# Other start addresses for the split weight buffers of a two-block float32 transformer kernel

## What is computed

```python
def first_block(x, ...):
    for i in range(DEPTH):
        h = rmsnorm(x, norm_mix[i])
        x = x + (even_mixer(h, ...) if i % 2 == 0 else odd_mixer(h, ...))
        x = x + conv_ffn(rmsnorm(x, norm_ffn[i]), ...)

def second_block(x, ...):
    for layer in range(DEPTH):
        x = x + hybrid_mixer(rmsnorm_2(x, norm1[layer]), ...)
        h = rmsnorm_2(x, norm2[layer])
        x = x + (swiglu(h, ...) if layer % 2 == 0 else moe_swiglu(h, ...))
```

## Time and profile before

| what | value |
|---|---|
| median of 2 runs | 1558.99 us (1557.62 to 1560.37) |
| the profiled execution, first to last instruction (span) | 1558.8 us |
| instructions | 26842, of them 9894 matmuls |
| PE busy | 1525.1 us (98%) |
| DVE busy | 1188.6 us (76%) |
| ACT busy | 1017.6 us (65%) |
| DMA | 351 MB, mean 225 GB/s |

### The profile page before, as it was taken

One profiled execution on the slowest core, in us unless ns is written; L12 is line 12 of the kernel. 1 busy time (PEld: TensorE's weight loads), 2 busy tenths in 40 slices (PEclk: granted clock), 3 DMA queues, 4 the chain that ended last, 5 costly groups with the idle time before them and its releaser, 6 DMA issues.

```text
span 1558.8 us, 26842 instructions
## 1 busy us (share of the span) xinstructions
PE 1525.1 (98%) x9894; PEld 1308.5 (84%) x9894; DVE 1188.6 (76%) x1477; ACT 1017.6 (65%) x1431; POOL 60.4 (4%) x74
## 2 busy tenths in 40 slices
PE   7999999999999999999999999999999999999998
PEld 6988888878878888899888888998878888888886
DVE  5677877775578877787775556887688888888887
ACT  5667665566567656687465455875577777777775
POOL 0000000000000000020000000100000001101000
PEclk9999999999999999999999999999999999999999
DMA  7535455445424555464255555462699999999995
GB/s 269 195 119 189 167 211 188 177 147 189 169 102 165 213 188 184 142 190 144 80 192 187 204 181 184 162 167 83 227 373 368 394 387 381 369 396 385 364 362 210
DMA packets 54794, 351.08 MB, mean 225 GB/s; under 512 B 6208, under 2 KB 9968, under 8 KB 14896
## 3 DMA queue, kind: packets, MB, share of 16 engines
q1 hardware_dynamic: 46512, 330.94, 56.8%
q0 software_dynamic: 8192, 18.90, 4.7%
HBM read 341.90 MB, written 7.91 MB: 224 GB/s over the span
## 4 chain that ended last, share of the span: by engine, by line
PE 91%; DVE 4%; DMA 2%; ACT 2%; issue 1%; POOL 0%; SPq 0%; DVEq 0%; ACTq 0%
PE PS L917 20%; PE PS L1852 16%; PE PS L1985 14%; PE PS L2021 11%; PE PS L1870 8%; PE PS L1986 8%; PE PS L1478 1%; DVE EWL L3761 1%; PE PS L1083 1%; PE PS L1956 1%; DMA rows_m<-HN 1%; PE PS L1833 1%; DMA W<-in_weights 1%; PE PS L962 1%; PE PS L1547 1%
## 5 line engine op out<-in xcount | busy, mean ns | idle before, releaser
L3761 DVE TENSOR_TENSOR EWL<-W,EWH 128x2048 fp32r<-128x2048 f32 x144 | 329.6, 2291 | 45.4 <-ACT EWH L2789 45.2
L1985 PE MATMUL PS<-HTB,WH 128*128 128x512 f32 x944 | 329.3, 393 | 0.0
L2789 ACT ACTIVATE EWH<-W 128x2048 fp32r<-128x2048 f32 x144 | 276.5, 1920 | 61.3 <-PE PS L1870 34.2
L1986 PE MATMUL PS<-HTB,WL 128*128 128x256 f32 x1008 | 282.4, 280 | 0.0
L3087 DVE TENSOR_TENSOR WL<-W,WH 128x2048 fp32r<-128x2048 f32 x99 | 226.5, 2287 | 35.9 <-ACT WH L2216 32.8
L2216 ACT ACTIVATE WH<-W 128x2048 fp32r<-128x2048 f32 x99 | 189.2, 1918 | 95.4 <-PE PS L1986 84.6
L917 PE MATMUL PS<-MWH,HTB 128*128 128x256 f32 (+1 forms) x940 | 240.9, 341 | 2.1 <-issue 1.5
L3095 DVE TENSOR_TENSOR MWL<-W,MWH 128x1024 fp32r<-128x1024 f32 x136 | 164.5, 1220 | 85.2 <-ACT MWH L2240 83.2
L1985 PEld LDWEIGHTS PS<-HTB,WH 128*128 128x128 f32 x944 | 177.2, 188 | 40.1
L2240 ACT ACTIVATE MWH<-W 128x1024 fp32r<-128x1024 f32 x136 | 142.5, 1054 | 98.2 <-PE PS L917 89.8
L1986 PEld LDWEIGHTS PS<-HTB,WL 128*128 128x128 f32 x1008 | 189.5, 188 | 1.0
(11 more groups left out here) (413 smaller groups left out, 2441.1 us busy)
## 6 DMA issues: line engine op xcount, KB each, us to landing
W<-in_weights SPq DMA_DIRECT2D x311, 1024.0 KB, 4.9
CS<-in_consts POOLq DMA_DIRECT2D x4, 403.5 KB, 4.8
ARENA<-rows_m POOLq DMA_DIRECT2D x8, 192.0 KB, 6.2
ARENA<-rows_m POOLq DMA_DIRECT2D x2, 768.0 KB, 12.2
moe_acc<-X POOLq DMA_DIRECT2D x3, 512.0 KB, 12.1
moe_rows<-HN POOLq DMA_DIRECT2D x3, 512.0 KB, 12.1
X<-in_x SPq DMA_DIRECT2D x2, 512.0 KB, 4.4
W<-in_weights SPq DMA_DIRECT2D x2, 512.0 KB, 7.1
```

Source lines behind the costliest of these rows:

```text
L1985: mm(PS[b][:, :], WH[:, sl, o:o + P], HTB[:, :, kk, :], start=(kk == 0), stop=False, skip_group_check=True)
L1986: ins = mm(PS[b][:, 0:256], WL[:, sl, o:o + P], HTH[:, kk, :], start=False, stop=(kk == KC - 1), skip_group_check=True)
L2789: A(EWH[tile % SPLIT][:, :], tile_ap(w0 + tile), ACT.Copy).then_inc(sem("moe_hi"), 1)
L3761: TT(EWL[tile % SPLIT][:, :], tile_ap(w0 + tile), EWH[tile % SPLIT][:, :].bitcast(F32), SUB).then_inc(sem("moe_lo"), 1)
```

## The change

Every split buffer gets a start of its own within 64 bytes. `shifted` allocates a buffer with 16 elements (64 bytes) of room and gives back the part that begins `by` elements in. The tuples are in elements of 4 bytes, one entry for each of the three buffers:

```diff
+SHIFT_ROOM = 16
+MIXER_SHIFT, FFN_SHIFT, MOE_SHIFT = (2, 4, 12), (12, 12, 4), (4, 6, 1)
...
+    nc.alloc_sbuf_tensor("HTB_END", [P, 2 * SHIFT_ROOM], F32)
     W = nc.alloc_sbuf_tensor("W", [P, RING, KC * TW], F32)
+    nc.alloc_sbuf_tensor("W_END", [P, 2 * SPLIT * SHIFT_ROOM], F32)
...
-    ARENA_N = 21632
+    ARENA_N = 21632 + 6 * SHIFT_ROOM
...
-    MWH = nc.alloc_sbuf_tensor_at("MWH", [P, SPLIT, HALF], F32R, offset=mw_at)
-    MWL = nc.alloc_sbuf_tensor_at("MWL", [P, SPLIT, HALF], F32R, offset=mw_at + 4 * SPLIT * HALF)
+    def shifted(name, n, at, by):
+        return nc.alloc_sbuf_tensor_at(name, [P, n + SHIFT_ROOM], F32R, offset=at)[:, by:by + n]
+    half_step = 4 * (HALF + SHIFT_ROOM)
+    MWH = [shifted(f"MWH{k}", HALF, mw_at + k * half_step, MIXER_SHIFT[k]) for k in range(SPLIT)]
+    MWL = [shifted(f"MWL{k}", HALF, mw_at + (SPLIT + k) * half_step, MIXER_SHIFT[k]) for k in range(SPLIT)]
...
+    WH = [shifted(f"WH{k}", KC * TW, wh_at + k * tile_step, FFN_SHIFT[k]) for k in range(SPLIT)]
+    WL = [shifted(f"WL{k}", KC * TW, wl_at + k * tile_step, FFN_SHIFT[k]) for k in range(SPLIT)]
...
-    EWH = [nc.alloc_sbuf_tensor_at(f"EWH{k}", [P, TILE_N], F32R, offset=o) for k, o in enumerate(moe_hi_at)]
-    EWL = [nc.alloc_sbuf_tensor_at(f"EWL{k}", [P, TILE_N], F32R, offset=o) for k, o in enumerate(moe_lo_at)]
+    EWH = [shifted(f"EWH{k}", TILE_N, o, MOE_SHIFT[k]) for k, o in enumerate(moe_hi_at)]
+    EWL = [shifted(f"EWL{k}", TILE_N, o, MOE_SHIFT[k]) for k, o in enumerate(moe_lo_at)]
```

More of the change, by code:

```diff
@@ L171, in build @@
     HT = nc.alloc_sbuf_tensor_at("HT", [P, KC, S], F32, offset=ht_at)
-    MWH = nc.alloc_sbuf_tensor_at("MWH", [P, SPLIT, HALF], F32R, offset=mw_at)
-    MWL = nc.alloc_sbuf_tensor_at("MWL", [P, SPLIT, HALF], F32R, offset=mw_at + 4 * SPLIT * HALF)
-    assert 2 * SPLIT * HALF <= (RING - RAW) * KC * TW
+    def shifted(name, n, at, by):
[3 more added lines that the diff above has]
+    MWL = [shifted(f"MWL{k}", HALF, mw_at + (SPLIT + k) * half_step, MIXER_SHIFT[k]) for k in range(SPLIT)]
+    assert 2 * SPLIT * HALF <= (RING - RAW) * KC * TW and max(MIXER_SHIFT + FFN_SHIFT + MOE_SHIFT) <= SHIFT_ROOM
     ff_n = 6 * 2 * 512
-    gh_n, wh_n = 2 * 512, SPLIT * KC * TW
+    gh_n, wh_n = 2 * 512, SPLIT * (KC * TW + SHIFT_ROOM)
     assert ff_n + 2 * gh_n + 2 * wh_n <= ARENA_N
@@ L179, in build @@
     GHL = nc.alloc_sbuf_tensor_at("GHL", [P, 2, 2, S], F32R, offset=arena_at + 4 * (ff_n + gh_n))
-    WH = nc.alloc_sbuf_tensor_at("WH", [P, SPLIT, KC * TW], F32R, offset=arena_at + 4 * (ff_n + 2 * gh_n))
-    WL = nc.alloc_sbuf_tensor_at("WL", [P, SPLIT, KC * TW], F32R, offset=arena_at + 4 * (ff_n + 2 * gh_n + wh_n))
-    WL1_AT = ff_n + 2 * gh_n + wh_n + KC * TW
+    tile_step = 4 * (KC * TW + SHIFT_ROOM)
+    wh_at, wl_at = arena_at + 4 * (ff_n + 2 * gh_n), arena_at + 4 * (ff_n + 2 * gh_n + wh_n)
+    WH = [shifted(f"WH{k}", KC * TW, wh_at + k * tile_step, FFN_SHIFT[k]) for k in range(SPLIT)]
+    WL = [shifted(f"WL{k}", KC * TW, wl_at + k * tile_step, FFN_SHIFT[k]) for k in range(SPLIT)]
+    WL1_AT = ff_n + 2 * gh_n + wh_n + KC * TW + SHIFT_ROOM
     TILE_N, sel_n, gr_n, xs_n = KC * TW, NT * N_EXP * P, 2 * 256, 2 * KC * P
     dead_at = -(-(cs_at + 4 * CST["reset"][0]) // 32) * 32
-    assert dead_at + 8 * TILE_N <= cs_at + 4 * (CST["pool"][0] + CST["pool"][1])
+    step_n = TILE_N + SHIFT_ROOM
+    assert dead_at + 8 * step_n <= cs_at + 4 * (CST["pool"][0] + CST["pool"][1])
     SELR = nc.alloc_sbuf_tensor_at("SELR", [P, NT, N_EXP, P], F32R, offset=arena_at)
     moe_hi_at = [dead_at, ht_at, arena_at]
-    moe_lo_at = [dead_at + 4 * TILE_N, htl_at, arena_at + 4 * TILE_N]
-    EWH = [nc.alloc_sbuf_tensor_at(f"EWH{k}", [P, TILE_N], F32R, offset=o) for k, o in enumerate(moe_hi_at)]
-    EWL = [nc.alloc_sbuf_tensor_at(f"EWL{k}", [P, TILE_N], F32R, offset=o) for k, o in enumerate(moe_lo_at)]
-    moe_at = arena_at + 4 * 2 * TILE_N
+    moe_lo_at = [dead_at + 4 * step_n, ht_at + 4 * step_n, arena_at + 4 * step_n]
+    EWH = [shifted(f"EWH{k}", TILE_N, o, MOE_SHIFT[k]) for k, o in enumerate(moe_hi_at)]
+    EWL = [shifted(f"EWL{k}", TILE_N, o, MOE_SHIFT[k]) for k, o in enumerate(moe_lo_at)]
+    moe_at = arena_at + 4 * 2 * step_n
     GRH = nc.alloc_sbuf_tensor_at("GRH", [P, 2, 256], F32R, offset=moe_at)
@@ L204, in build @@
     GAT = nc.alloc_sbuf_tensor_at("GAT", [P, NT, GAT_W], F32R, offset=moe_at + 4 * (2 * gr_n + 2 * xs_n + S))
-    moe_n = 2 * TILE_N + 2 * gr_n + 2 * xs_n + S + gat_n
+    moe_n = 2 * step_n + 2 * gr_n + 2 * xs_n + S + gat_n
     sel_at = -(-mx_at // 32) * 32
@@ L209, in build @@
     GAIN = nc.alloc_sbuf_tensor_at("GAIN", [P, D], F32, offset=sel_at)
-    YL = [nc.alloc_sbuf_tensor_at(f"YL{k}", [P, D // 2], F32R, offset=o) for k, o in enumerate((sel_at + 4 * D, dead_at + 8 * TILE_N))]
-    assert sel_at + 6 * D <= mx_at + 4 * N_MX and dead_at + 8 * TILE_N + 2 * D <= cs_at + 4 * CST["before"][0]
+    YL = [nc.alloc_sbuf_tensor_at(f"YL{k}", [P, D // 2], F32R, offset=o) for k, o in enumerate((sel_at + 4 * D, dead_at + 8 * step_n))]
+    assert sel_at + 6 * D <= mx_at + 4 * N_MX and dead_at + 8 * step_n + 2 * D <= cs_at + 4 * CST["before"][0]
     PS = [nc.alloc_psum_tensor(f"PS{b}", [P, 512], F32) for b in range(8)]
@@ L546, in build @@
     od.QN = v3(a(1024), 2)
+    a(SHIFT_ROOM)
     od.SM = a(2 * 1152).rearrange("p (u g k) -> p u g k", u=2, g=3)
@@ L995, in first_channel_half @@
                     o = k * TW + c * P
-                    ins = mm(bank(key)[:, c * 256:(c + 1) * 256], MWH[:, hf, o:o + P], HTL[:, 4 * hf + k, :], start=False,
+                    ins = mm(bank(key)[:, c * 256:(c + 1) * 256], MWH[hf][:, o:o + P], HTL[:, 4 * hf + k, :], start=False,
                              stop=(hf == 1 and k == KC // 2 - 1), skip_group_check=True)
@@ L1955, in first_units @@
                         for n_w, wt in enumerate((WH, WL)):
-                            mm(PS[4 + c][:, 0:256], wt[:, sl, o:o + P], HTH[:, kk, :], start=(kk == 0 and n_w == 0),
+                            mm(PS[4 + c][:, 0:256], wt[sl][:, o:o + P], HTH[:, kk, :], start=(kk == 0 and n_w == 0),
                                stop=(kk == KC - 1 and n_w == 1), skip_group_check=True)
@@ L1962, in first_units @@
                         o = kk * TW + c * P
-                        ins = mm(PS[4 + c][:, 256:512], WH[:, sl, o:o + P], HTL[:, kk, :], start=False, stop=(kk == KC - 1),
+                        ins = mm(PS[4 + c][:, 256:512], WH[sl][:, o:o + P], HTL[:, kk, :], start=False, stop=(kk == KC - 1),
                                  skip_group_check=True)
@@ L1981, in up @@
                             if parted(gs, i):
-                                mm(PS[b][:, 0:256], WH[:, sl, o:o + P], HTH[:, kk, :], start=(kk == 0), stop=False, skip_group_check=True)
-                                mm(PS[b][:, 0:256], WH[:, sl, o:o + P], HTL[:, kk, :], start=False, stop=False, skip_group_check=True)
-                            else:
-                                mm(PS[b][:, :], WH[:, sl, o:o + P], HTB[:, :, kk, :], start=(kk == 0), stop=False, skip_group_check=True)
-                            ins = mm(PS[b][:, 0:256], WL[:, sl, o:o + P], HTH[:, kk, :], start=False, stop=(kk == KC - 1),
+                                mm(PS[b][:, 0:256], WH[sl][:, o:o + P], HTH[:, kk, :], start=(kk == 0), stop=False, skip_group_check=True)
+                                mm(PS[b][:, 0:256], WH[sl][:, o:o + P], HTL[:, kk, :], start=False, stop=False, skip_group_check=True)
+                            else:
+                                mm(PS[b][:, :], WH[sl][:, o:o + P], HTB[:, :, kk, :], start=(kk == 0), stop=False, skip_group_check=True)
+                            ins = mm(PS[b][:, 0:256], WL[sl][:, o:o + P], HTH[:, kk, :], start=False, stop=(kk == KC - 1),
                                      skip_group_check=True)
@@ L1996, in last_quarter @@
                             o = c * D + 512 + 256 * part
-                            ins = mm(out, gh[:, gs % 2, c, P:2 * P], wt[:, sl, o:o + 256], start=(part == 1 and c == 0 and n == 0),
+                            ins = mm(out, gh[:, gs % 2, c, P:2 * P], wt[sl][:, o:o + 256], start=(part == 1 and c == 0 and n == 0),
                                      stop=(c == 1 and n == 2), skip_group_check=True)
@@ L2215, in hi @@
                     await_full(act, ("od", "o", 3))
-            A(WH[:, j % SPLIT, :], tile_ap(t), ACT.Copy).then_inc(hi_done, 2)
+            A(WH[j % SPLIT], tile_ap(t), ACT.Copy).then_inc(hi_done, 2)
         def ffn_ahead(mixer):
@@ L2231, in hi_half @@
             if name == "ev" and h < 2:
-                A(rank_half(MWH[:, h, :]), rank_half(half_ap(name, h)), ACT.Copy).then_inc(hi_done, 1)
+                A(rank_half(MWH[h]), rank_half(half_ap(name, h)), ACT.Copy).then_inc(hi_done, 1)
                 return
@@ L2239, in hi_half @@
                     act.wait_ge(half_used, firsts_before[name] + u // 2 + 1)
```

(2 more changed lines are left out.)

16 lines of the change are left out of this document (8 added, 8 removed).

## The result

| | before | after |
|---|---|---|
| median of the runs | 1558.99 us (1557.62 to 1560.37, 2 runs) | 1568.94 us (1568.27 to 1569.61, 2 runs) |
| ratio | | 1.0067, 95% interval 1.005 to 1.0083 |
| profiled execution, span | 1558.8 us | 1566.5 us (its own time is 1568.27, 1.8 us around the span) |

The change costs 0.7%. The forecast was 1544, 15 us faster; the result is 10 us slower and lies 3 us above the range that was given (1512 to 1566), near the "slower" rival's 1570, which had a chance of 0.13.

The account below looks back on a forecast made before the run. PE was taken to bound the kernel through the distance between matmuls. The experts' 11.4 us in full plus 3.4, a quarter of the other 13.7, made 15 us off 1558.8, so 1544 us, with an 8 in 10 range of 1512 to 1566.

Parts of the forecast that it names:

- "slower" rival: Feed-forward down and mixers' 512-column matmuls lose a favourable 0.227 us level for 0.234; 1570 if half do, 1581 all; chance 0.13.
- What bounds the kernel: Whole kernel: PE, busy 98% and 91% of the chain, so the distance between matmul starts sets the time.
- The distance depends on the relative place of the two operands: PE's matmuls: relative place of moving and stationary operand moves the cost by some ns, in either direction.
- Nearest rows: All matmuls: 0.224 us at 512 columns, 0.118 at 256, together 25 us gained, of which 15 were taken.
- favourable-lock rival: The slower case: both operands at one place give 0.227 us, any other place 0.234; 1570 or 1581, chance 0.13.
- the experts' 11.4 us: Experts' up and down matmuls: 1152 x 5 = 5.8 us and 564 x 10 = 5.6 us gained, taken in full.
- the upper end: All 512-column matmuls at the dearest steady level seen, 0.234 us, 256-column ones at 0.120; together 22 us lost.
- Much faster: Rival for PE's matmuls, gain several times as large, shown by mixers' 256-column distance below 0.116 us; chance 0.22.
- Nothing moves: Rival for the whole kernel: the starts don't matter and the chain's pieces stay unchanged; chance 0.20.
- ACT, DVE and DMA at nothing: Experts' stage: split times on ACT and DVE don't count (0 to 0.23 us each), and transfers don't set the pace.

Follow-up runs that it names:

- sweep: Whole computation left out, PE alone, 48 matmuls for each of 23 pairs of operand starts at 512 and 256 columns; 226.9 to 239.4 ns at 512 columns.
- sweepbusy: The same PE-only matmuls over 23 pairs of starts, while ACT copies and DVE subtracts 2048 columns again and again; PE's 2350 matmuls 409.3 us for 409.4.
- zero: The changed kernel with all shifts set to 0, its 64-byte rooms kept; 1563.13 us, ratio 1.0028 to the kernel before.
- room256: The layout of before with 256 bytes of room behind each mixer and feed-forward buffer, no shifts; 1559.23 us, ratio 0.9999 to the kernel before.
- sweepfar: Whole computation left out, PE alone, 25 pairs of places up to 2048 bytes, bases a multiple of 8192 apart; 226.7 to 227.7 ns in step at 512 columns.

## Why the prediction was wrong

- **What bounds the kernel:** right. PE's chain share even rose, and with 26842 instructions unchanged the result is read from one number per kind of matmul in the counted pieces.
- **The distance depends on the relative place of the two operands, by some ns in either direction:** right. `sweep` shows it with the other engines idle, 226.9 to 239.4 ns at 512 columns and 116.9 to 123.1 at 256; in `sweepbusy`, with DVE 81% and ACT 69% busy, the distances are the same to 0.2 ns behind the first pair.
- **The step that failed, first half: "Nearest rows".** It took a passing 0.22 us, read as 0.224, as the price of places that the trace didn't show, and then counted the experts' 11.4 us in full. What stood against it was in the prediction itself: the favourable-lock rival needed one comparison (228 against 234 ns) and that comparison was at hand. The value was the shortest in a stretch where distances wander after a disturbance. The experts up went to 234 ns instead of 224 (1152 by 5 = 5.8 us lost instead of 5.8 won) and the experts down to 235 to 237 instead of 224. So the experts' term came out as 6.1 us lost for 11.4 won. In the feed-forward down the sign was wrong too, 232 for 224, and in the mixers' 512 columns, 233 for 224. Only for the mixers' 256 columns was it right, 118 for 120.
- **The step that failed, second half: the price of what "moves up by multiples of 64 bytes".** It was never costed, since only the place within 64 bytes was taken to matter. `zero` measured it, by itself, at 4 us (the whole change loses 10), and `room256` showed that a room of 256 bytes has no cost.
- **The bounds:** the upper end, 22 us with every 512-column matmul at 0.234, held as a sum; the result is 45% of it. Its level was not a bound: the experts down went to 235 to 237, and `sweep` has places at up to 239.4. The range left out the far third of the slower case, and the result fell just there.
- **The slower rival:** right in that a favourable level is lost (its test, the feed-forward's down piece at 5.6, reads 5.56) and close in size, 1570 against 1568.94. It had 0.13. Its "both at one place" within 64 bytes is not what makes the level: `zero` kept that and lost it. And its size, half of 22 us, was a guess that came out near.
- **Much faster:** falls. Its chance of 0.22 and the range's lower end, 1512, rest on the author's estimate of what a matmul takes when nothing is in its way, and no run shows such a level. Of 48 pairs in the sweeps none came below 226.7 ns at 512 columns and 114.0 at 256.
- **Nothing moves:** falls.
- **ACT, DVE and DMA at nothing:** right, by unchanged durations and 275.0 us of waits of SyncE for 276.6.

Open: what repeats every 256 bytes. The runs show the dependence, not its cause. Also open is why the kernels' distances off the good level are smaller or larger than the sweep's at the same difference, and so what each place of the change should cost by itself. For the mixers the direction is shown by the pieces, but the stages' lengths differ from one execution to the next by as much.

## What to carry to other kernels

In a kernel bound by one-pass float32 matmuls of 512 columns that load new weights each time, put the moving and the stationary operand on multiples of 32 bytes and a multiple of 256 bytes apart (`sweepfar` has 226.7 to 228.1 ns there and 229.0 to 237.7 at all other pairs), and look at every pad and room between them: rooms of 64 bytes cost 0.3% here, and 32 bytes in the right place won 0.3%. Divide the counted pieces of the chain before and after a change of layout; a few ns per matmul show there first. And when no row shows a new place, the level at which the kernel runs steadily is better evidence than the best moment in it; a steady good level that depends on addresses is something that a move can lose.

## What the runs showed of the hardware that was not expected

- The distance of matmuls has a period of 256 bytes in the difference of the operands (0, 256, 512, 1024 and 2048 at 227.1 to 227.7 ns, 64 and 320 both at 229.0). That is four times the 64 bytes that the change reckons with.
- An equal start is not enough: both at 4 gives 237.7 ns, both at 32 gives 228.1.
- The best place depends on the columns. With 256 columns, in step is a slow level, 120 ns, and the moving operand 192 bytes up gives 114.0. This isn't a matter of the difference alone: the stationary operand 64 bytes up, the same difference modulo 256, gives 117.9 (5.66 / 48). A layout of this kind for the mixers' and the feed-forward's 256-column matmuls wasn't tried.
- In `sweep` the place (28, 0), a difference of 156 bytes modulo 256, reached 226.9 ns, though it is on no multiple of 32. In `sweepbusy` it did so again. Its chain there, the pair (4, 0) and then (28, 0):

```profile
35.92 11.32 PE PS L67 x48
...
103.85 10.89 PE PS L67 x48
```

  The rule of 256 and 32 doesn't explain this one, so it is a rule for finding the good level and not a full account of it.
